# Adaptive-norm rows spread through device memory, constant matmuls in TensorE's stops, and turned queries and keys copied ahead of two exponentials

## The reference, cut to what matters

```
cond = silu(c)
mod = cond @ w_ada + b_ada                       # one row of 6 * 1024
shift1, scale1, gate1, shift2, scale2, gate2 = split(mod, 6)
h = modulate(x, norm1_w, shift1, scale1)
x = x + gate1 * hybrid_mixer(h, ...)             # dilated attention and a gated delta rule, then w_out
h = modulate(x, norm2_w, shift2, scale2)
x = x + gate2 * routed_moe(h, ...)               # 32 experts, top 4
```

```
a_low = strict_lower(kb @ k.T * decay);  lhs = a_low + I
u, w  = triangular_solve(lhs, vb), triangular_solve(lhs, kb * exp(gc))
intra = (q @ k.T) * decay
```

## Time and profile before

| what | value |
|---|---|
| timed runs, median (lowest to highest) | 2227.36 us (2224.89 to 2227.48) |
| profiled execution, its own time | 2219.78 us |
| its span | 2218.0 us |
| PE busy | 2117.4 us (95%) |
| DVE busy | 973.6 us (44%) |
| ACT busy | 333.6 us (15%) |
| mean granted clock of TensorE | 0.992 of 2.4 GHz |
| chain that ended last: PE, DMA, DVE | 63%, 29%, 5% of the span |

### The profile page before, as it was taken

The page is one execution under the profiler, slowest core; times in us unless marked ns, Lnnn a source line. Parts: engine busy times, 40 slices in busy tenths (PEclk is TensorE's granted clock), DMA queues, the critical chain, the costliest instruction groups (busy, mean ns, idle before and its releaser), DMA issues.

```text
span 2218.0 us, 23806 instructions
## 1 busy us (share of the span) xinstructions
PE 2117.4 (95%) x9694; PEld 1161.9 (52%) x9700; DVE 973.6 (44%) x1523; ACT 333.6 (15%) x737; POOL 48.3 (2%) x30
## 2 busy tenths in 40 slices
PE   6998999999999999999999999999999999999999
PEld 4855743333233233333233365886885557868874
DVE  1455534333332233332332225853677256725684
ACT  1123110000000000000000021321110113311110
POOL 0000100000000000000000001100000011000000
PEclk9998999999999999999999999999999999999999
DMA  9556079999999999999999764334443534343441
GB/s 372 198 221 270 18 249 402 428 429 429 428 428 429 428 429 429 428 429 428 428 429 428 314 234 159 126 111 137 152 152 133 178 116 153 113 146 121 153 162 65
DMA packets 132861, 603.38 MB, mean 272 GB/s; under 512 B 9238, under 2 KB 65734, under 8 KB 104122
## 3 DMA queue, kind: packets, MB, share of 16 engines
q1 hardware_dynamic: 132794, 602.43, 68.4%
HBM read 601.34 MB, written 3.16 MB: 273 GB/s over the span
## 4 chain that ended last, share of the span: by engine, by line
PE 63%; DMA 29%; DVE 5%; ACT 1%; issue 1%; POOL 1%; SPq 0%; POOLq 0%; DVEq 0%
DMA ring<-in_w_dram 28%; PE bank L601 21%; PE bank L1366 12%; PE bank L611 8%; PE bank L2379 6%; PE bank L2342 3%; PE bank L814 2%; PE bank L2357 2%; PE bank L2722 1%; DMA ring<-in_w_ada_dram 1%; PE bank L538 1%; PE bank L1420 1%; PE bank L1347 1%; PE bank L2293 1%; PE bank L592 1%
## 5 line engine op out<-in xcount | busy, mean ns | idle before, releaser
L1366 PE MATMUL bank<-ring,arena 128*64 128x512 f32 x3168 | 706.3, 596 | 37.1 <-DMA ring<-in_w_dram 35.7
L601 PE MATMUL bank<-hTbuf,ring 128*128 128x256 f32 x2368 | 516.0, 380 | 2.8 <-ACT hTbuf L2611 2.6
L1366 PEld LDWEIGHTS bank<-ring,arena 128*64 128x64 f32 x3168 | 217.4, 137 | 515.0 <-issue 417.0
L601 PEld LDWEIGHTS bank<-hTbuf,ring 128*128 128x128 f32 x2368 | 450.1, 191 | 67.1 <-issue 5.9
L1069 DVE TENSOR_SCALAR arena<-bank 128x512 f32<-128x512 f32 x33 | 22.8, 692 | 412.6 <-PE bank L1366 412.6
L611 PE MATMUL bank<-ring,hTbuf 128*128 128x512 f32 (+2 forms) x384 | 151.2, 554 | 0.0
L2032 DVE SCALAR_TENSOR_TENSOR arena<-bank,arena 128x254 f32<-128x254 f32 (+1 forms) x176 | 76.7, 477 | 84.7 <-ACT arena L2176 83.1
L611 PEld LDWEIGHTS bank<-ring,hTbuf 128*128 128x128 f32 x384 | 72.6, 190 | 75.1 <-issue 71.8
L1073 DVE RECIPROCAL arena<-arena 128x512 f32<-128x512 f32 x33 | 110.7, 3353 | 1.1
L1193 ACT ACTIVATE arena<-arena 128x512 f32<-128x512 f32 x33 | 20.8, 629 | 547.0 <-DVE arena L1069 547.0
L1093 DVE TENSOR_TENSOR arena<-bank,arena 128x512 f32<-128x512 f32 x33 | 22.8, 692 | 127.0 <-PE bank L1366 127.0
(11 more groups left out here) (430 smaller groups left out, 1838.6 us busy)
## 6 DMA issues: line engine op xcount, KB each, us to landing
ring<-in_w_dram SPq DMA_DIRECT2D x198, 2048.0 KB, 24.0
ring<-in_w_up_dram SPq DMA_DIRECT2D x44, 1024.0 KB, 6.7
ring<-in_w_in_dram SPq DMA_DIRECT2D x21, 2048.0 KB, 7.8
ring<-in_w_ada_dram SPq DMA_DIRECT2D x12, 2048.0 KB, 9.0
ring<-in_w_down_dram SPq DMA_DIRECT2D x10, 2048.0 KB, 7.8
ring<-in_w_out_dram SPq DMA_DIRECT2D x6, 2048.0 KB, 8.5
ring<-in_w_in_dram SPq DMA_DIRECT2D x4, 1024.0 KB, 14.0
ring<-in_w_proj_a_dram SPq DMA_DIRECT2D x2, 2048.0 KB, 8.0
```

The source lines that it names most:

```text
L601: ins = pe.matmul(B.bank(name, j)[:, i * T:(i + 1) * T], w[:, k, (first + i) * P:(first + i + 1) * P], hT[:, k, :], start=(k == 0), stop=( ...
L1366: ins = pe.matmul(bank[g * SLOTS:(g + 1) * SLOTS, :], lhsT, rhs[:, g * CH:(g + 1) * CH], start=start, stop=stop)
```

## The change

Four edits.

1. `ada_t` and `ada_s` go. The four rows of each group, one from each 32 partitions of `ada_rows`, are written to device memory (`mod_rows`) and read back into all partitions of `mod` by one DMA each way, both issued by SyncE (`spread`). Group 1's pair stands ahead of the bias table's DMA, group 2's between it and the expert chunks; SyncE waits for the write to land before it issues the read. The readers wait for the flags `mod_in1` and `mod_in2`. ScalarE waits for the first write before it overwrites `ada_rows`.
2. ScalarE's copies of `ag2` and of the four `fm` banks come ahead of the wait for `row` and the two exponentials.
3. `keep_running` is put at four stops of TensorE: 10 products ahead of `t0`, 9 ahead of `gc`, 4 ahead of the `kk` products, 13 ahead of `p2`.
4. The banks `ad1` and `ad2` leave the plan, so the names between them move by four banks; from `fm` on they are where they were.

```diff
-    ... ("s0", 2), ("s1", 4), ("ag1", 1), ("ad1", 4), ("t0", 2), ...
-    ... ("row", 2), ("ag2", 1), ("ad2", 4), ("fm", 4), ...
+    ... ("s0", 2), ("s1", 4), ("ag1", 1), ("t0", 2), ...
+    ... ("row", 2), ("ag2", 1), ("fm", 4), ...
...
-        def ada_t(pe, g):
-            ada_rows_t(pe, g)
-            for due in B.all_taken((f"ag{g}", 1), room=(f"ad{g}", 0)):
-                pe.wait_ge(*due)
-            for i in range(4):
-                ...
-                pe.matmul(B.bank(f"ad{g}", i)[:], ident[:, 32 * i:32 * i + 1].to_broadcast([P, P]), ada_rows, start=True,
-                          stop=True).then_inc(B.full(f"ad{g}", i), 1)
...
-        def ada_s(act, g):
-            ada_rows_s(act, g)
-            for i in range(4):
-                act.wait_ge(*B.ready(f"ad{g}", i))
-                act.activation(mod[:, (4 * g + i) * CH:(4 * g + i + 1) * CH], B.bank(f"ad{g}", i)[:], ACT.Copy)\
-                   .then_inc(B.free(f"ad{g}", i), 1)
+        def spread(sp, g):
+            sp.wait_ge(*B.taken(f"ag{g}"))
+            sp.dma_start(mod_rows[g - 1], ada_rows[0:P:32, :]).then_inc(S["mod_out"], 16)
+            sp.wait_ge(S["mod_out"], 16 * g)
+            sp.dma_start(mod[:, 4 * g * CH:4 * (g + 1) * CH], mod_rows[g - 1].rearrange("i n -> (i n)").partition_broadcast(P))\
+              .then_inc(S[f"mod_in{g}"], 16)
...
             act.activation(erem[:, 0, :], sp_a[:, 0, :], ACT.Exp).then_inc(S["gexp"], 1)
+            act.wait_ge(S["mod_out"], 16)
+            ada_rows_s(act, 2)
+            for j in range(4):
+                act.wait_ge(*B.ready("fm", j))
+                act.activation(tile4((QTn, KTn)[j // 2], j % 2), b4("fm", j), ACT.Copy).then_inc(B.free("fm", j), 1)
             act.wait_ge(*B.taken("row", 1))
             act.activation(Am, Am, ACT.Exp, scale=-1.0)
             act.activation(DTm, DTm, ACT.Exp).then_inc(S["dmat"], 1)
-            ada_s(act, 2)
-            for j in range(4):
-                act.wait_ge(*B.ready("fm", j))
-                act.activation(tile4((QTn, KTn)[j // 2], j % 2), b4("fm", j), ACT.Copy).then_inc(B.free("fm", j), 1)
...
+            pe.wait_ge(*B.room("gc"))
+            keep_running(pe, B.bank("gc"), 9)
             pe.wait_ge(S["gb"], 1)
-            pe.wait_ge(*B.room("gc"))
...
-            ada_t(pe, 2)
+            ada_rows_t(pe, 2)
             for j in range(4):
                 pe.wait_ge(S["kqn"], j // 2 + 1)
                 four("fm", j, ...)
+            pe.wait_ge(*B.room("kk"))
+            keep_running(pe, B.bank("kk"), 4)
...
+            pe.wait_ge(*B.room("p2"))
+            keep_running(pe, B.bank("p2"), 13)
             pe.wait_ge(S["e_mat"], 2)
...
-            pe.wait_ge(*B.taken("ad1", 3))
+            pe.wait_ge(S["mod_in1"], 16)
             pe.wait_ge(*B.room("shc"))
...
-            v.wait_ge(*B.taken("ad2", 3))
+            v.wait_ge(S["mod_in1"], 16)
+            v.wait_ge(S["mod_in2"], 16)
...
+            spread(sp, 1)
             sp.wait_ge(S["rel_row"], 16)
             sp.dma_start(scratch..., row8...).then_inc(S["rel_out"], 16)
+            spread(sp, 2)
             for ch in range(RING):
...
-            ada_s(act, 1)
+            ada_rows_s(act, 1)
             silu_s(2)
...
-            ada_t(pe, 1)
+            ada_rows_t(pe, 1)
+            pe.wait_ge(*B.room("t0"))
+            keep_running(pe, B.bank("t0"), 10)
```

More of the change, by code:

```diff
@@ L228, in split @@
     return ap.rearrange("p (a b) -> p a b", a=n)
-FLAGS = [
+FLAGS = ["mod_out", "mod_in1", "mod_in2",
     "first_in", "x_in", "con_in", "small_in", "mod_c",
@@ L305, in build_program @@
         banks = [ctx.enter_context(nc.psum_tensor(f"bank{b}", [P, CH], F32)) for b in range(8)]
+        mod_rows = nc.dram_tensor("mod_rows", (2, 4, CH), F32, kind="Internal").ap()
         row8 = nc.dram_tensor("bias_row", (8, REL), F32, kind="Internal").ap()
@@ L441, in ada_rows_t @@
             ins.then_inc(B.full(f"ag{g}"), 1)
-        def ada_t(pe, g):
-            ada_rows_t(pe, g)
-            for due in B.all_taken((f"ag{g}", 1), room=(f"ad{g}", 0)):
-                pe.wait_ge(*due)
-            for i in range(4):
-                if i:
-                    pe.wait_ge(*B.room(f"ad{g}", i))
-                pe.matmul(B.bank(f"ad{g}", i)[:], ident[:, 32 * i:32 * i + 1].to_broadcast([P, P]), ada_rows, start=True,
-                          stop=True).then_inc(B.full(f"ad{g}", i), 1)
         def ada_rows_s(act, g):
```

## The result

The changed kernel's median is 2213.41 us over 4 runs (2212.01 to 2214.94), before's 2226.12 us (2224.84 to 2227.48). The ratio is 0.9943, interval 0.9927 to 0.9959: 12.7 us faster, where 8.7 were forecast. The profiled execution tells another size: its span is 2213.1 us, only 4.9 us shorter than the 2218.0 of before's. Both differences have to be explained.

What follows compares the result with a forecast made beforehand. The prediction took the chain through TensorE, VectorE and ScalarE as the bound up to the expert stage's weight stream; 8.2 + 0.5 = 8.7 us off the median 2227.36 gave 2218.7 us, range 2214.5 to 2224.

Steps and rivals of the forecast that it cites:

- Broadcasts and order: Delta rule: without broadcasts and with fm copied ahead of the exponentials, VectorE's first kk step starts 8.2 us earlier.
- The overlap of `aT`: Delta rule: the aT transposes no longer stand behind the kk and kq products on TensorE, gaining 0.5 us.
- The DMAs: SyncE's write and read of the modulation rows land well before their readers: cost 0, up to 13 us without cover.
- The constants: Constant products ahead of t0, gc, kk and p2 fit into TensorE's waits: cost at full clock 0.
- the clock held behind `gc`: The nine constant products prevent the clock's fall at 180, bringing the group 2 rows from 195.5 to 190.5.
- B: Rival: the clock falls all the same behind gc; gain only 3.7 to 5.3 us, time 2222.9, chance 0.17.
- the last one of the sum: End of the sum: the 8.7 us gain was taken off the timed median 2227.36, giving 2218.7 us.
- Group 1's broadcasts: Attention: they stood while VectorE computed and TensorE waited for it afterwards, so removing them gains 0 on the path.
- Rival E: Ahead of p2: timed runs may have a clock fall there; thirteen constants give up to 3 us more, 2215; no separate chance.
- the fall in the attention: At t0, near 163: ten constants come too early, the clock's fall stays; taken as 0, bounds 0.6 gain, 0.8 loss.
- D: Rival: slower, because the clock falls in the stretch from p2 to xl; time 2232, chance 0.06.
- C: Rival: nothing measurable moves, something unseen follows close behind, the weight stream above all; time 2227, chance 0.12.

Runs made afterwards that it cites:

- e12: The kernel before, unchanged, profiled a third time: span 2218.7 us, mean clock 0.992.
- e1: The kernel before, unchanged, profiled and timed again: 2225.34 us, ratio 0.999, span 2224.5 us.
- f2: The kernel before, unchanged, a fourth profile: 2224.66 us, ratio 1.0002, span 2224.4 us.
- e2: The changed kernel, unchanged, run again: 2213.88 us, ratio 0.9943, span 2213.4 us.
- f1: The changed kernel, unchanged, once more in the fourth batch: 2214.23 us, ratio 0.9952, with before at 2222.94 us.
- e8: The changed kernel with ScalarE's copies of ag2 and fm put back behind the two large exponentials: 2219.67 us, ratio 0.9974.
- e6: The changed kernel without the thirteen constant products ahead of p2: 2213.14 us, ratio 0.9947.
- e3: The changed kernel without all four runs of constant products: 2219.75 us over 7 runs, ratio 0.9967.
- e7: The changed kernel without the ten constant products ahead of t0: 2213.53 us, ratio 0.9945.
- e9: The changed kernel without constants and with ScalarE's order of before, leaving only the transfer through device memory: 2221.44 us, ratio 0.9993 to before.
- f3: The changed kernel without all four runs of constant products, again in the fourth batch: 2214.07 us, ratio 0.9952.
- e11: The changed kernel with shc, br and VectorE's u and w products moved into the stops, and constants among the ab products: 2204.37 us, ratio 0.9917.
- f4: The kernel of e11 again, in the fourth batch: 2206.91 us, ratio 0.992.

## Why the prediction was wrong in size

The pieces of seven profiles, worked out from the start times of the rows in their timelines (us; kk is VectorE's first step on it):

```
                   scores  t0-scores  gc-t0  kk-gc  p2-kk  shc-p2  wo-shc  span
before              140.4     21.4    18.1   25.5    6.7    35.5    15.7   2218.0
before, e12         138.9     21.4    18.1   25.5    6.7    35.5    17.4   2218.7
before, e1          140.9     22.9    17.4   27.2    6.7    37.1    17.2   2224.5
before, f2          139.2     22.9    17.4   27.4    6.7    37.1    18.8   2224.4
after               140.8     21.7    17.5   17.2    6.0    35.5    18.8   2213.1
after, e2           141.2     21.6    17.5   17.2    6.0    35.5    17.2   2213.4
after, f1           141.1     21.6    17.5   17.2    6.0    35.5    17.2   2212.4
```

**The steps of the sum were right against the execution that they were read from.** *Broadcasts and order*: 8.2 forecast, 25.5 - 17.2 = 8.3 measured. The overlap of `aT`: 0.5 forecast, 0.6 measured. e8 shows that the new order carries 4.8 of it. The DMAs cost nothing, and their cover was enough. The constants fit, and the clock held behind `gc` in all three profiles after, so B did not come.

**The step that failed is the last one of the sum**: "against the median 2227.36 - 8.7 = 2218.7 us. I take this." I had noted that the profiled execution was 7.6 us faster than the median and took the difference as a constant. It isn't. Before has two kinds of executions, and the profile was of the faster one. In the second (e1, f2) the clock fell where the thin `ab` products end and stayed at half until 153 to 155, which stretches t0-scores by 1.5 us; it fell again at the broadcasts (kk-gc longer by 1.7 to 1.9) and behind the start of `p2` (shc-p2 longer by 1.6). The change removes the first two with the broadcasts, and no profile after has the third. So against an execution of the second kind it takes off 22.9 - 21.6 = 1.3, 27.3 - 17.2 = 10.1, 0.6 and 1.6 us, less 0.1 for gc-t0: 13.5 up to `shc`; the spans differ by 11.0 to 12.1. Against one of the first kind it is 4.6 to 6.3 at the end, because the forecast left out that the `shc` to `w_out` piece can cost more (3.0 us in the first profile after, 1.4 in e2 and f1).

Smaller terms go with this. "*Group 1's broadcasts* [...] Taking them away gives nothing on the path: 0" holds for the first kind only; in the second it is 1.3 us. Rival E, which the sum put at nothing, came in the second kind: its fall begins 1.3 to 1.5 us behind the start of `p2`, behind the stop that the thirteen constants fill, and costs 1.6 us up to `shc`, where up to 3 were given; e6 has such a fall without them. And the fall in the attention, which the prediction expected to stay, went: gc-t0 is 17.5 us where the first profile had 18.1, the 0.6 that it gave as a bound. All four profiles without the broadcasts and without the ten constants (e3, e7, e9, f3) have a fall there, at 159 to 165, and none of the seven with them in which the scores ran at half clock (e7's gc-t0 is 18.5). Where the scores ran at full clock (e11, f4), the ten constants were over at 156.6 and 155.0, the fall came at 158.8 and 157.2 in spite of them, and gc-t0 is 18.6: there they do come too early.

**Before's spread goes with the clock.** Over the 101 executions of before in the four batches, from 2217.1 to 2230.1 us, the time falls by 2.1 us for each 0.001 of mean granted clock. They lie in two heaps, 37 below 2223 us (median 2220.8) and 64 above (median 2226.4); the execution profiled first (2219.78) belongs to the lower heap, the three timed ones behind 2227.36 to the upper. 0.001 of 2226 us is 4.5 us more at half clock, so nearly half of each such microsecond, all that half clock costs, would lie on the path; this is a correlation, not an experiment. The changed kernel's 15 executions lie between 2210.5 and 2215.4 at a mean clock of 0.993. Its gain came out as 12.7, 12.6 and 8.7 us on three occasions because before's median moved (2226.1, 2226.4, 2222.9), not its own (2213.4, 2213.9, 2214.2). That a first median of three executions, all of the upper heap, stood against a profile of the lower one was chance.

**What stays open.** What the constants are worth. In profiles the thirteen do what they are for: the fall behind the start of `p2` stands in five of the eight profiles without them (e1, f2, e6, e9, f3: `p2` to `shc` 36.85 to 37.1 us, else 35.4 to 35.5) and in none of the seven with them. But up to `w_out` that leaves little: 53.3 us on average without them, 52.7 with them. In the ratios to before, the transfer alone has 0.9993 (e9), with the constants 0.9974 (e8), with the new order 0.9967 and 0.9952 (e3, f3), with both 0.9943, 0.9943 and 0.9952. So the constants seem to be worth about 4 us in the old order and 6 or 0 in the new one; the intervals of each pair overlap, and e8 and e9 come from different batches. With constants the spread is smaller (5 us against 11.5 in e3 and f3 together); that the constants cause it, and not the batches, is argued and not shown. What decides between before's kinds at 137 to 141 is not known; chip 8 shows both heaps in its timed executions. The new order alone, with the broadcasts still there, and taking away group 1's broadcasts alone were not tried.

D (slower) and C (nothing moves) did not come: SyncE's second pair of chunks moved from 286.03 to 280.27 with `w_out`, and the end with them.

## What to carry to other kernels

Sum a change against several executions, not one: where the granted clock of two profiles differs, note each stretch at half clock that lies on the chain and ask of each whether the change keeps it, before carrying the sum over to a median. An order in which one engine serves two consumers can be worth as much as the work itself: copying first what the other engine needs earliest gave 6 of the 12 us, for no instruction, and taking away the broadcasts without it and without constants gave nothing. Fill a stop with work that is on the path later rather than with constants: moving `shc`, `br` and VectorE's products into the stops brought 2207, and with constants among the `ab` products 2204 to 2207, which in the one batch with both was 7.3 us below the changed kernel. How these 7 us divide between TensorE's and VectorE's moved work was not tried.

## What the runs showed of the hardware

- TensorE's clock fell while the engine was busy all the time: at 138.9 us in the first profile, in `ab` (8 columns, from 136.1), and within 1.8 us before to 0.8 us behind the end of `ab` in all sixteen profiles without constants there. With a 512-column constant behind every second k of `ab` it held until 158.8 (e11) and 157.2 (f4).
- It fell in `shc` or `br` (1 and 32 columns, behind a stop of 0.90 us) in all fifteen profiles where they stand ahead of `u0`, at 240.5 to 254.3 us, and not there in the three where they are moved; in those it fell at 194.7 to 196.3 instead, in the products behind `shc`.
- Behind a stop of 3.2 us ahead of `p2` it fell in five of eight profiles, within 0.3 us before to 1.5 us behind the start of `p2`. With the stop filled but for 0.35 to 0.41 us it fell there in none of seven.
- One and the same program has executions that differ by 13 us (0.6%), and the time falls by 2.1 us for each 0.001 of mean granted clock.
- An 8 KB write on a queue with weights in front of it held up its issuing engine for 4.67 us at the issue, and 13.9 us passed until the read behind it could be issued; issued at 191.90, when the 2 MB of the bias table in front of it were nearly through (issued at 183.47, landed after 9.4 us), the same pair took 1.7 us from issue to issue. The read of 8 KB into 128 partitions (1 MB) landed in 4.8 us.
